# Two merge-gate groups multiplied during the last attention steps, their projections later, in a planned eight-core decoder trunk

## The chip, the cores and the metric

The kernel runs on the eight cores of one Trainium2 chip. Each core takes one of the eight sequences of the batch and shares nothing with the others but the weights that all of them read from device memory. The metric is device time in microseconds (us), of the slowest of the eight cores; lower is better. Engines are named as in the profile: PE multiplies matrices (PEld is its loading of weights), DVE does elementwise arithmetic, ACT evaluates functions, POOL and SP here mostly issue transfers.

## The reference, cut to what matters

Two layers, each on x of 2048 tokens by 2048 channels per core:

```python
shift, scale, gate = split(c_act @ w_ada + b_ada)          # adaLN: one vector each per sequence
h    = x * (1 + scale) + shift
proj = h @ w_in                                            # all mixer inputs, and 4 x 2048 merge-gate logits
ys   = (ssd_branch(..), swa_branch(..), shortconv_branch(..), rglru_branch(..))   # A, B, C, D: 1024 channels each
gates = sigmoid(merge.reshape(b, l, 4, d) + b_gate)
m    = sum(gates[:, :, i] * (ys[i] @ w_branch[i]) for i in range(4))
x    = layer_norm(ALPHA * x + gate[:, None] * (m @ w_out))
```

A is a Mamba-2 mixer (SSD) over chunks of 128 tokens, B is attention over a window of 128 tokens with 16 heads and rotary embedding (rope), C is a gated convolution, D a linear recurrence.

## The kernel before

**Units and stages.** A core works through four units: layer 0 on tokens 0 to 1023 and 1024 to 2047, then layer 1 on the same halves. A unit has these stages, and in all of them PE also has large projections to do: the inputs of mixers C and D; the SSD of mixer A, between whose small steps the first merge pass runs (gates and projections of C and D, groups `m0_0` to `m15_0`); attention, in eight pairs of heads (`qg0` to `qg7`); the second merge pass (gates and projections of A and B, groups `m0_1` to `m15_1`); and `m @ w_out` with its layer norm (`out_unit`, `out_last`). A layer norm runs on into the next unit's first stage.

**A group.** A projection of 256 channels over 1024 tokens is done by `wino` with seven products instead of eight, of two times four matmuls of 128x128 by 128x512 each ("a half" is four such matmuls). After the products, in turn, the four results `c11`, `c22`, `c12` and `c21` are taken out of PSUM by ACT and DVE. For a merge group, `use` makes the gate (tanh) of each result, and `fill` multiplies the matching piece of a mixer's output by `w_branch`, which `mix` joins with the gate. `fill` is called by `wino` right behind each result, so a merge group holds its PSUM bank and its turn until the mixer's output is there.

**Attention's last tiles.** The outputs of mixer A, and of B's first four head pairs, are parked in device memory (`yd_scr`, `yb_scr`) and fetched back by `yload` on SP's queue, as 16 and 8 tiles, before the second merge pass. `rope` swaps halves of a head over partitions by four small transfers (SBUF to SBUF, `arena<-arena`) and then multiplies on DVE.

**adaLN.** Of layer 1's 96 pieces of `w_ada` (and 32 of layer 0's gate) each is one 512 KB transfer on SP's queue and two DVE multiply-adds; after eight pieces `ada_fin` sums over partitions with four small matmuls on PE. `ada_bg(cnt, step)` spreads them: 64 pieces, one each 15 us, in units 0 and 1.

**What sets the order.** The order of every engine's instructions is fixed when the program is built. `Prog.live` plays the program through with fixed costs per operation and per transfer (`DMA_RATE`, `DMA_LAT`, `SLACK`) and lets each free engine take the ready operation of the smallest key. A key is a planned time within the unit (`k0 + TC + ...`) less an advance (`HI`); generators such as `mg`, `yload` or `ada_bg` hand over work when the plan comes to their key. On the chip each engine goes through its list in that order, and waits on semaphores where a predecessor isn't done. All tiles are parts of one tensor `arena`, and PSUM is `ps`, so the profile's names are `arena` and `ps`; lines L705, L709, L713 are the helpers of ACT activations, DVE tensor-tensor and DVE multiply-add operations, L736 and L741 those of matmuls and transposes, L329 that of transfers.

The softmax here doesn't subtract the row's maximum and nothing guards it: scores larger than these inputs give would overflow.

## Time and profile before

| | us |
|---|---|
| median of 3 runs | 5914.43 (5913.79 to 6663.6) |
| profiled execution, its own time | 5964.13 |
| its span on the slowest core, core 7 | 5963.1 |
| PE busy in that span | 5615.3 (94%) |
| DVE busy | 4187.6 (70%) |
| ACT busy | 2842.6 (48%) |
| weight loads on PE | 2570.3 |

The page is of the slowest core. All four units are read from one profiled execution: unit 0 runs from about 152 to 1644 us, unit 1 to 3112, unit 2 to 4526 and unit 3 to the end. The first 150 us load adaLN and x, with little for PE to do. In a table of stretches, the stretch's length less the PE's busy time is PE's idle time; PEclk is the granted share of full clock.

### The profile page before, as it was taken

Reading aid. Unit: us, or ns where it says so; the run is one execution under the profiler, and the core shown is the slowest. Engines: PE = TensorE matmul, PEld = TensorE weight load, DVE = VectorE, ACT = ScalarE, POOL = GpSimd, SP = SyncE. Lnnn points to the kernel's source line nnn. Section 1 sums busy time; section 2 is a strip of 40 time slices with the busy share of each in tenths; the row PEclk is TensorE's granted clock in tenths of the full one; section 3 lists DMA queues with packets and bytes.
Section 4 is the critical chain, followed back from the end, with each engine's and each line's share of the span. In section 5 each row is a group of like instructions: output and inputs, shape, how many; then the busy total and the mean of one; then the engine's idle time right before and its main releaser. Section 6 shows DMA issues by size and latency. Waiting matters only on the chain.

```text
span 5963.1 us, 85339 instructions; the slowest of 8 cores (5863.3 to 5963.1 us)
## 1 busy us (share of the span) xinstructions
PE 5615.3 (94%) x28680; PEld 2570.3 (43%) x28680; DVE 4187.6 (70%) x6902; ACT 2842.6 (48%) x4518; POOL 323.0 (5%) x563
## 2 busy tenths in 40 slices
PE   1999888989999998999999999999999999998998
PEld 1444434434444444444444444444444444443445
DVE  7787866756588787775668767766558767776556
ACT  1565654433156565443326656644324656644224
POOL 0000000000000000000000000000000000000004
PEclk9999999999999999999999999999999999999999
DMA  9667767577566575767656566766756556665554
GB/s 300 124 134 138 145 131 169 131 168 182 166 159 132 122 149 134 163 141 181 157 173 146 97 110 126 134 134 137 181 165 156 106 94 115 118 137 114 115 117 148
DMA packets 251823, 856.94 MB, mean 144 GB/s; under 512 B 27776, under 2 KB 91392, under 8 KB 206848
## 3 DMA queue, kind: packets, MB, share of 16 engines
q0 software_dynamic: 64672, 411.20, 40.1%
q1 hardware_dynamic: 184416, 423.51, 23.6%
q10 hardware_dynamic: 2304, 16.78, 0.9%
q8 instruction: 234, 3.83, 0.3%
q14 instruction: 197, 1.61, 0.1%
HBM read 1133.32 MB, written 120.85 MB: 210 GB/s over the span
## 4 chain that ended last, share of the span: by engine, by line
PE 86%; DMA 5%; DVE 4%; issue 3%; ACT 2%; SPq 1%; DVEq 0%; ACTq 0%; POOL 0%; POOLq 0%
PE ps L736 85%; ACT arena L705 2%; DVE arena L709 2%; DMA arena<-w_ada 2%; DVE arena L713 2%; DMA arena<-arena 1%; PE ps L741 1%; SPq L329 1%; DMA mp_scr<-arena 0%; DMA arena<-x 0%; DMA arena<-cum_scr 0%; DMA arena<-wb 0%; DMA yd_scr<-arena 0%; ACT L705 0%; DMA arena<-yb_scr 0%
## 5 line engine op out<-in xcount | busy, mean ns | idle before, releaser
L736 PE MATMUL ps<-arena 128*128 128x512 bf16 (+6 forms) x27976 | 5588.4, 367 | 315.3 <-DVE arena L709 104.8
L736 PEld LDWEIGHTS ps<-arena 128*128 128x128 bf16 (+3 forms) x27976 | 2510.7, 101 | 3303.6 <-issue 817.9
L709 DVE TENSOR_TENSOR arena<-arena 128x1024 bf16<-128x1024 bf16 (+9 forms) x3052 | 1991.9, 689 | 271.3 <-ACT arena L705 161.3
L705 ACT ACTIVATE arena<-arena 128x512 f32<-128x512 f32 (+9 forms) x2356 | 1395.2, 633 | 1403.4 <-DVE arena L709 814.9
L709 DVE TENSOR_TENSOR arena<-ps,arena 128x512 f32<-128x512 f32 (+5 forms) x1491 | 707.7, 492 | 571.8 <-PE ps L736 496.0
L705 ACT ACTIVATE arena<-ps 128x512 f32<-128x512 f32 (+4 forms) x838 | 534.8, 645 | 668.9 <-PE ps L736 565.5
L713 DVE SCALAR_TENSOR_TENSOR arena<-arena 128x1024 f32<-128x1024 f32 (+3 forms) x765 | 760.0, 1005 | 114.2 <-ACT arena L705 66.8
L713 DVE SCALAR_TENSOR_TENSOR arena<-arena,ps 128x512 f32<-128x512 f32 (+1 forms) x640 | 403.9, 642 | 577.3 <-PE ps L736 528.1
L705 ACT ACTIVATE ps<-ps 128x512 f32<-128x512 f32 x624 | 363.6, 583 | 573.3 <-PE ps L736 524.0
L705 ACT ACTIVATE arena<-ps,arena 128x512 f32<-128x512 f32 (+1 forms) x456 | 312.3, 685 | 347.2 <-PE ps L736 318.6
L705 ACT ACT_TABLE_LOAD x238 | 305.4, 1283 | 99.9 <-DVE arena L709 50.9
L329 POOL DMA_DIRECT2D arena<-w x184 | 97.7, 531 | 2728.7 <-PE ps L736 2003.9
L713 DVE SCALAR_TENSOR_TENSOR arena<-ps,arena 128x512 f32<-128x512 f32 (+1 forms) x153 | 104.9, 687 | 160.5 <-PE ps L736 157.6
L329 POOL DMA_DIRECT2D arena<-wg x128 | 67.7, 529 | 2054.8 <-PE ps L736 1962.4
L709 DVE TENSOR_TENSOR ps<-ps,arena 128x512 f32<-128x512 f32 (+1 forms) x222 | 147.6, 665 | 13.6 <-ACT arena L705 0.5
L741 PE MATMUL ps<-arena 128*128 128x128 bf16 (+1 forms) x704 | 102.0, 245 | 15.9 <-DVE arena L709 11.6
L329 POOL DMA_DIRECT2D arena<-wb x128 | 67.8, 531 | 704.2 <-DVE arena L709 290.4
L741 PEld LDWEIGHTS ps<-arena 128*128 128x128 bf16 (+1 forms) x704 | 69.2, 116 | 72.2 <-issue 31.0
L709 DVE TENSOR_TENSOR arena<-arena,ps 128x256 f32<-128x256 f32 (+1 forms) x172 | 74.7, 445 | 22.6 <-PE ps L736 18.4
L727 DVE RECIPROCAL arena<-arena 128x4 f32<-128x4 f32 (+3 forms) x144 | 72.4, 504 | 11.7 <-ACT arena L705 5.6
L709 POOL TENSOR_TENSOR arena<-arena 128x256 f32<-128x256 f32 (+1 forms) x81 | 71.6, 909 | 97.4 <-ACT arena L705 96.7
L1604 DVE TENSOR_TENSOR_SCAN arena<-arena 128x1024 f32<-128x1024 f32 x32 | 74.1, 2314 | 0.7
(18 smaller groups left out, 85.0 us busy)
## 6 DMA issues: line engine op xcount, KB each, us to landing
arena<-w POOLq DMA_DIRECT2D x184, 1024.0 KB, 10.0
arena<-wg POOLq DMA_DIRECT2D x128, 1024.0 KB, 10.1
arena<-w_ada SPq DMA_DIRECT2D x128, 512.0 KB, 7.3
arena<-wb POOLq DMA_DIRECT2D x128, 512.0 KB, 11.1
arena<-x SPq DMA_DIRECT2D x64, 512.0 KB, 5.4
mp_scr<-arena SPq DMA_DIRECT2D x64, 512.0 KB, 8.4
arena<-cum_scr SPq DMA_DIRECT2D x128, 256.0 KB, 7.3
arena<-mp_scr SPq DMA_DIRECT2D x64, 512.0 KB, 10.8
```

The source lines that it names most:

```text
L329: eng.dma_start(out=o.fn[0], in_=o.fn[1]).then_inc(s, 16)
L705: return P.op("act", lambda e: e.activation(out=out, in_=in_, func=func, **kw), reads, writes, cost=cost, acc=acc, tbl=tbl, hi=hi)
L709: return P.op(eng, lambda e: e.tensor_tensor(out=out, in0=in0, in1=in1, op=op), reads, writes, cost=0.2 + n * 2.1e-3 if eng == "pool" else ...
L713: return P.op("dve", lambda e: e.scalar_tensor_tensor(out=out, in0=in0, scalar=scalar, in1=in1, op0=op0, op1=op1), reads, writes, cost=c_d ...
L727: P.op("dve", lambda e: e.reciprocal(out=out, in_=in_), reads, writes, cost=0.13 + n * 6.3e-3)
L736: r = e.matmul(out, lhsT=lhsT, rhs=rhs, start=st, stop=sp_, skip_group_check=True)
L741: P.op("pe", lambda e: e.transpose(out=out, in_=in_, identity=ident), reads, writes, cost=cost, acc=acc)
L1604: P.op("dve", lambda e: e.tensor_tensor_scan(out=c, data0=a, data1=xs, initial=init, op0=ALU.mult, op1=ALU.add), [ra, rxs] + ri, cv.r, cos ...
```

## The change

It does six things. The planner's transfer rate goes from 280 to 325 GB/s, so it takes every transfer as shorter. `ROPEL` goes from 8 to 0: rope's multiplies, which wait for the swap transfers, get a key that is 8 us earlier. `LNSTEP` goes from 9 to 7: the layer norm of one unit is handed out faster into the next unit's start. `ada_bg` hands out 48 pieces each 20 us in unit 0, 64 each 15 us in unit 1 and 16 each 24 us in unit 2, instead of 64 and 64. The first two groups of the second merge pass (`dc < LAZY`) get a key 30 us earlier (`M1E`). And these two no longer call `fill` in `wino`: a generator `later` calls it for the four results in turn, once the gate of each is there. `LATEM` is empty and changes nothing. The rest of the arithmetic is the same, and each engine has as many operations as before. The whole order is planned anew.

```diff
-    DMA_RATE = 280e3
+    DMA_RATE = 325e3
...
-    ROPEL, HL, ADAL = 8.0, 6.0, 15.0
+    ROPEL, HL, ADAL = 0.0, 6.0, 15.0
...
-        cons = {"c11": c11, "c22": lambda c, q, r: use(1, 1, c, q, r, ALU.add),
+        cons = {"c11": c11, "has": lambda k: SLOT[k] in G, "c22": lambda c, q, r: use(1, 1, c, q, r, ALU.add),
...
-    LNSTEP = 9.0
+    LNSTEP = 7.0
...
+    LAZY = 2
+    M1E = 30.0
+    ADAN = ((48, 20.0), (64, 15.0), (16, 24.0))
...
         def mg(k, dc, p):
             cons, fill, load = merge(l, n, dc, p)
-            group(k, "m%d_%d" % (dc, p), wg_in[l, dc, p], cons, 2.8, fill)
+            if p and dc < LAZY:
+                done = cons.pop("done")
+
+                def later():
+                    for q in ("c11", "c22", "c12", "c21"):
+                        while not cons["has"](q):
+                            yield POLL
+                        yield from fill(q)
+                        yield P.key + 2.8
+                    done()
+                go(later(), k + 2.0)
+            group(k, "m%d_%d" % (dc, p), wg_in[l, dc, p], cons, 2.8, None if p and dc < LAZY else fill)
             go(load(), k - 20.0)
...
-            mg(k0 + TC + s2 * dc, dc, 1)
+            mg(k0 + TC + s2 * dc - (M1E if dc < LAZY else 0.0), dc, 1)
...
-        if n < 2:
-            go(ada_bg(64, 15.0), k0 + 30.0)
+        if n < 3:
+            go(ada_bg(*ADAN[n]), k0 + 30.0)
```

**Place 1: PE, seventh head pair of unit 0.** In PE's list, 128x256 and the following 128x128 on L736 are products of queries and keys (QK), 128x65 are products of the probabilities with the values (PV), L741 128x128 are transposes of the result, and 128x512 are halves of projections. Before:

```order
L736 MATMUL ps<-arena 128x65 x6
L736 MATMUL ps<-arena 128x256 x4
L741 MATMUL ps<-arena 128x128 x2
L736 MATMUL ps<-arena 128x128 x2
L736 MATMUL ps<-arena 128x65 x10
L736 MATMUL ps<-arena 128x256 x2
L741 MATMUL ps<-arena 128x128 x4
L736 MATMUL ps<-arena 128x256 x4
L736 MATMUL ps<-arena 128x512 x4
```

The same steps now, from the QK of four key blocks on:

```order
L736 MATMUL ps<-arena 128x256 x4
L736 MATMUL ps<-arena 128x512 x4
L736 MATMUL ps<-arena 128x65 x8
L736 MATMUL ps<-arena 128x512 x8
L736 MATMUL ps<-arena 128x65 x2
L736 MATMUL ps<-arena 128x512 x8
L741 MATMUL ps<-arena 128x128 x2
L736 MATMUL ps<-arena 128x512 x4
L736 MATMUL ps<-arena 128x65 x6
L736 MATMUL ps<-arena 128x128 x2
L736 MATMUL ps<-arena 128x512 x4
L741 MATMUL ps<-arena 128x128 x2
```

Halves of `m0_1` and `m1_1` have moved in between these steps, where seven rows stood with none.

**Place 2: PE, the first wait for the tiles that `yload` fetches, unit 0.** `s_dve` and `s_act` are waits for DVE and ACT, `d_sp_` numbers are waits for transfers on SP's queue, here the tiles of `yd_scr`, and `d_pool_` one on POOL's. Before, the wait stood behind the last transposes of the last head pair:

```order
L741 MATMUL ps<-arena 128x128 [waits s_dve]
L741 MATMUL ps<-arena 128x128
L736 MATMUL ps<-arena 128x512 x4
L736 MATMUL ps<-arena 128x512 [waits s_act]
L736 MATMUL ps<-arena 128x512 x7
L736 MATMUL ps<-arena 128x512 [waits d_sp_49,d_sp_47,d_sp_45,d_sp_43,d_pool_2]
L736 MATMUL ps<-arena 128x512 x3
L736 MATMUL ps<-arena 128x512 [waits d_sp_50,d_sp_48,d_sp_46,d_sp_44]
```

Now it stands within the last head pair's steps, ahead of its third QK:

```order
L741 MATMUL ps<-arena 128x128 [waits s_dve]
L741 MATMUL ps<-arena 128x128
L736 MATMUL ps<-arena 128x512 [waits d_sp_33,d_sp_31,d_sp_29,d_sp_27,d_pool_0]
L736 MATMUL ps<-arena 128x512 x7
L736 MATMUL ps<-arena 128x256 [waits s_act]
L736 MATMUL ps<-arena 128x256 x3
L736 MATMUL ps<-arena 128x65 [waits s_dve]
L736 MATMUL ps<-arena 128x65 x7
```

The transposes at the head of the second fence are those of the seventh head pair's end, not the eighth's: the wait has moved forward past most of one head pair. From the QK in place 1 on, 64 matmuls of 128x512 stood ahead of it, and 40 do now.

**Place 3: PE, third group of heads in the SSD of unit 0.** L741 128x128 are the transposes that open a chunk, 128x256 on L736 is the product that makes a chunk's state, which needs what DVE makes of those transposes, 128x1 is `ada_fin`. Before:

```order
L736 MATMUL ps<-arena 128x512 x8
L736 MATMUL ps<-arena 128x1 x4
L741 MATMUL ps<-arena 128x128 x2
L736 MATMUL ps<-arena 128x128
L736 MATMUL ps<-arena 128x256
L741 MATMUL ps<-arena 128x128 x2
L736 MATMUL ps<-arena 128x128
L736 MATMUL ps<-arena 128x512 x32
```

Now:

```order
L736 MATMUL ps<-arena 128x512 x4
L741 MATMUL ps<-arena 128x128 x2
L736 MATMUL ps<-arena 128x128
L736 MATMUL ps<-arena 128x512 x20
L736 MATMUL ps<-arena 128x256
L736 MATMUL ps<-arena 128x512 x8
L741 MATMUL ps<-arena 128x128 x2
L736 MATMUL ps<-arena 128x128
```

Between the transposes of chunk 5 and the product of its state there are five halves now, and there were none; `ada_fin` stands elsewhere.

## Rows read from the trace of the kernel before

**Rows 1.** Span and mean granted clock: the slowest core, and each die's median.

```profile
core 7: 5963.1 us, clock 0.971
die 0 (median of its cores): 5902.5 us, clock 0.983
die 1 (median of its cores): 5938.7 us, clock 0.976
```

**Rows 2.** Busy time by stretch, SSD of units 0 to 3, and the columns.

```profile
core 7: us, PE busy (x) PEld busy (x) DVE busy (x) ACT busy (x) POOL busy (x), PEclk, DMA share, GB/s
468.30:955.80 487.50, 431.34 (x2148) 197.46 (x2147) 355.91 (x630) 272.11 (x490) 22.93 (x44) 0.93 0.71 141
...
1980.00:2434.10 454.10, 421.52 (x2160) 193.86 (x2159) 355.86 (x617) 273.71 (x508) 18.75 (x36) 0.96 0.65 138
...
3431.70:3858.50 426.80, 411.00 (x2113) 188.76 (x2112) 313.06 (x557) 269.65 (x493) 22.91 (x44) 0.97 0.68 122
...
4845.90:5261.90 416.00, 409.41 (x2135) 188.76 (x2134) 318.15 (x553) 273.63 (x510) 18.74 (x36) 0.98 0.63 115
```

**Rows 3.** The same view, last two head pairs to the third merge group, units 0 to 3.

```profile
1158.40:1262.10 103.70, 81.72 (x478) 36.87 (x476) 66.32 (x141) 36.24 (x48) 4.23 (x8) 0.87 0.69 166
...
2637.40:2729.60 92.20, 78.00 (x472) 35.90 (x471) 61.05 (x128) 35.83 (x47) 4.78 (x9) 0.91 0.74 171
...
4056.50:4142.80 86.30, 77.11 (x453) 34.65 (x452) 54.51 (x117) 35.13 (x47) 4.24 (x8) 0.92 0.74 165
...
5469.50:5560.80 91.30, 75.99 (x463) 34.51 (x462) 56.56 (x116) 36.04 (x47) 4.22 (x8) 0.91 0.68 154
```

**Rows 4.** The same view: second merge pass of unit 0, and starts of units 1 and 2.

```profile
1262.10:1644.60 382.50, 382.46 (x1888) 175.40 (x1887) 224.83 (x367) 108.92 (x170) 13.19 (x25) 1.00 0.69 173
1644.60:1980.00 335.40, 326.73 (x1478) 139.41 (x1477) 288.70 (x366) 201.07 (x280) 13.20 (x25) 0.94 0.64 142
...
3112.90:3431.70 318.80, 316.25 (x1461) 135.46 (x1460) 254.70 (x318) 197.10 (x265) 16.28 (x31) 0.97 0.61 120
```

**Rows 5.** In order of time, unit 0's seventh head pair: start, us, instruction, [idle before <-releaser].

```profile
1197.07 1.02 ACT L705 ACTIVATE arena<-ps 128x1024 bf16<-128x1024 f32 x1
...
1200.46 3.17 DVE L709 TENSOR_TENSOR arena<-arena 128x1024 f32<-128x1024 f32 x4 [3.15 <-DMA arena<-arena]
...
1202.43 0.71 PE L736 MATMUL ps<-arena 128*128 128x65 bf16 x10 [3.90 <-DVE arena L709]
...
1203.68 0.68 DVE L709 TENSOR_TENSOR arena<-arena 128x1024 bf16<-128x1024 bf16 x1
```

**Rows 6.** In order of time, SP's queue at the same place (rope's copies, `yload`).

```profile
1191.53 2.37 SPq L329 DMA_DIRECT2D arena<-arena  x4
...
1208.29 15.98 SPq L329 DMA_DIRECT2D arena<-yd_scr  x16
1224.31 3.75 SPq L329 DMA_DIRECT2D arena<-yb_scr  x8
```

**Rows 7.** Transfers issued from 1200 to 1245 us: median time to landing last.

```profile
arena<-yd_scr SPq DMA_DIRECT2D x16, 128.0 KB, 11.4
```

**Rows 8.** Waits from 1190 to 1245 us: total, times, longest.

```profile
PE ps L736 <- DMA arena<-yb_scr: 7.5, 1, 7.5
```

**Rows 9.** Busy time by stretch, within the SSD of unit 0.

```profile
800.00:850.00 50.00, 27.63 (x127) 12.20 (x125) 31.90 (x65) 21.88 (x43) 0.50 (x1) 0.73 0.38 95
```

**Rows 10.** Waits from 800 to 850 us.

```profile
PE ps L736 <- DVE arena L713: 8.6, 2, 7.4
...
DVE arena L713 <- DMA arena<-w_ada: 6.0, 1, 6.0
```

**Rows 11.** The chain of waits at that place: start, us, what.

```profile
788.73 21.30 DMA arena<-w_ada
```

**Rows 12.** DVE's groups by shape, rope's and adaLN's: count | busy, mean ns | idle before.

```profile
L709 DVE TENSOR_TENSOR arena<-arena 128x1024 f32<-128x1024 f32 x240 | 289.0, 1218 | 48.3 <-DMA arena<-arena 38.0 <-ACT arena L705 9.9
...
L713 DVE SCALAR_TENSOR_TENSOR arena<-arena 128x512 f32<-128x512 f32 x374 | 276.9, 744 | 42.4 <-DMA arena<-w_ada 27.8 <-DVE arena L713 2.8 <-DVE arena L709 0.3
```

**Rows 13.** Busy time by stretch: two short ones at a lower granted clock.

```profile
286.25:292.69 6.44, 6.44 (x27) 2.68 (x25) 5.37 (x7) 5.06 (x8) 0.00 (x0) 0.81 0.94 163
842.74:849.57 6.83, 3.00 (x14) 1.30 (x15) 4.87 (x9) 3.69 (x9) 0.00 (x0) 0.50 0.00 1
```

More of the change, by code:

```diff
@@ L1641, in locked @@
         return g()
+    SLOT = {"c11": (0, 0), "c22": (1, 1), "c12": (0, 1), "c21": (1, 0)}
     def merge(l, n, dc, p):
@@ L1663, in fill @@
         def fill(k):
-            i, ti = {"c11": (0, 0), "c22": (1, 1), "c12": (0, 1), "c21": (1, 0)}[k]
+            i, ti = SLOT[k]
             while "wb" not in G or any(ydone[b] < 8 * (n + 1) for b in ((1, 4) if pair[i] == 1 else (pair[i],))):
@@ L2046, in build_program @@
     GX = (6, 7)
+    LATEM = ()
+    LAZY = 2
+    M1E = 30.0
+    ADAN = ((48, 20.0), (64, 15.0), (16, 24.0))
     groups = []
@@ L2104, in mg @@
             cons, fill, load = merge(l, n, dc, p)
-            group(k, "m%d_%d" % (dc, p), wg_in[l, dc, p], cons, 2.8, fill)
+            if p and dc < LAZY:
[9 more added lines that the diff above has]
+            group(k, "m%d_%d" % (dc, p), wg_in[l, dc, p], cons, 2.8, None if p and dc < LAZY else fill)
             go(load(), k - 20.0)
         for dc in range(16):
-            mg(k0 + TA + 12.0 + SM * dc, dc, 0)
+            mg(k0 + TA + 12.0 + SM * dc if dc < 16 - len(LATEM) else k0 + TC + LATEM[dc - 16], dc, 0)
         def dopen(m):
```

## The prediction

> **What bounds the kernel now.** I read the cores first: core 7 is the slowest, and its die has the lower clock [rows 1]. Then I cut its span by stages and took each stretch's PE busy time from its length. The second merge pass shows what the kernel does at its best: of 382.50 us PE idles 0.04, at granted clock 1.00, 382.46 us for 1888 matmuls, so 0.203 us a matmul and 0.81 us a half [rows 4]. PE bounds that stretch, and nothing but fewer matmuls would shorten it. Idle time sits elsewhere. The SSD of units 0 to 3 has 56.2, 32.6, 15.8 and 6.6 us of it (111.2), the ends of attention 22.0, 14.2, 9.2 and 15.3 (60.7) [rows 2, 3]. The number of matmuls is nearly the same in each of the four, so work does not explain the differences. Units 0 and 1 carry the adaLN pieces, 2 and 3 none. In these stretches PE waits for chains through ACT and DVE: the chain, not a busy engine, sets the pace. Since every matmul has to be done anyway and the merge pass behind has no gap, a microsecond of idle time removed ahead of it comes off the end, and none can be made good there.
>
> Two things add to it. The granted clock of the four ends is 0.87, 0.91, 0.92 and 0.91, against 1.00 in the merge pass [rows 3, 4]; stretches at 0.50 (1.2 GHz) lie behind idle time, as at 842.74 us [rows 13]. And DVE goes through its list in order, so a late transfer in it stops everything behind it: rope's multiplies waited 38.0 us for their swaps, adaLN's 27.8 us for `w_ada` [rows 12].
>
> **The change, part by part.** All sums are made on the profiled execution, 5964.13 us; the median of the runs is 49.7 us lower, and I take off the same microseconds there.
>
> *Ends of attention.* One step from QK to PV takes 1.02 us on ACT and 0.68 us on DVE [rows 5], with the handing over some 2.3 us, my estimate. Place 1 had no halves in seven rows; now one or two (0.81 to 1.62 us) stand between most dependent steps. That covers between a third and two thirds of a step, and where DVE itself is late, as at 1202.43, where PE idled 3.90 us behind a swap [rows 5], it covers only its own length. Bounds: nothing, if DVE stays the one that is late; all 60.7 us. I take 60%, nearer to the step than to the late swap: **-36 us**. The clock: missing share times PE busy time is 0.13 x 81.72 + 0.09 x 78.00 + 0.08 x 77.11 + 0.09 x 75.99 = 30.6 us [rows 3]; part of the low clock lies in idle time, so I count half, and 60% of it goes: **-9** (0 to -31).
>
> *The new wait.* Place 2 is what speaks against the change. PE's first wait for the `yd_scr` tiles now stands inside the last head pair's steps, and that pair's QK, PV and transposes are queued behind it; ACT and DVE then wait for those. Before, the tiles were issued over 15.98 us from 1208.29 on [rows 6] and took 11.4 us [rows 7]. The wait needs the seventh of 16, issued at about 1208.3 + 6/16 x 16.0 = 1214.3, landed at about 1225.7. PE came to it at about 1228, some 25 matmuls before the 7.5 us that it then waited for `yb_scr` until 1240.7 [rows 8]. Now 40 rather than 64 matmuls of projections stand between place 1 and the wait: 24 x 0.203 = 4.9 us earlier, and up to 14 us earlier as the 9 us of gaps at place 1 close too. With 2 us in hand, that is 3 to 12 us of waiting, if the tiles are issued no earlier. They may be: rope's last swaps were issued at 1191.53 [rows 6], 16.8 us before the tiles, and the tiles stand right behind them in the list but for two or three transfers; then the wait is 0. Bounds 0 to 12 us a unit; I take 5, near the middle: **+20** over four units. As a price from a page, the Trainium skill (DMA: Bandwidth & Descriptors, Anatomy of one DMA) has a fixed cost of about 2 us and 436 GB/s: a 128 KB tile would land in about 2.3 us, an estimate by that page, and this term would be nothing. The trace does not agree: 11.4 us is the median here, with the other transfers beside it.
>
> *SSD of units 0 and 1.* The 50 us from 800 on hold 22.4 us of unit 0's 56.2 [rows 9]. 7.4 of them are `ada_fin` behind a `w_ada` piece that landed 21.30 us after its issue [rows 10, 11]; the rest are steps that stood without a half between them, as in place 3, and there now are five halves. So 22.4 - 7.4 = 15 go. The other 33.8 us go with the pieces: 48 in place of 64 in unit 0, a quarter: 8.5. Unit 1 keeps 64 pieces and gets a replanned order: 4 of its 32.6. Together **-27** (between 0, if new late pieces take their place, and -76, if both came to unit 3's 6.6). The clock (0.93 and 0.96, partly at 0.81) gives back about a quarter of 0.07 x 431 = 30: **-7**.
>
> *Sixteen adaLN pieces in unit 2.* Their DVE work (two multiply-adds of 0.744 us each [rows 12], 24 us in all) lies beside PE's projections; unit 1's start, with pieces, idles 8.7 us, unit 2's, without, 2.6 [rows 4]. About 20 pieces cost 6.1, so 16 cost **+5** (0 to 5).
>
> *Layer norm in 7 us steps.* DVE is busy 288.70 of 335.40 us at the start of unit 1 [rows 4], and the same work is handed out in 112 rather than 144 us. It is covered while PSUM is emptied in time; without that cover the 8.7 us could double in three units. I take **+3** (0 to 26).
>
> *Rope's key.* The multiplies now stand at the first place at which the plan has the swaps landed, with less other DVE work ahead of them. The waits were 38.0 us [rows 12]. Bounds: none more, or as much again. I take half, 19 us on DVE, of which 40% reaches PE, as halves now stand between: **+8**.
>
> *Transfer rate, opening, output.* The merge passes and the output projection have no PE idle time to lose or win; their cover is the weights' lead of 70 us in the plan. The opening keeps its transfers, and I cost it at nothing (3 us either way).
>
> **The sum** is -36 - 9 + 20 - 27 - 7 + 5 + 3 + 8 = -43 us: 5921 us on the profiled execution, 5914.4 - 43 = **5871 us** as a median, 0.7% less.
>
> **The rivals.** *The gain is eaten.* The new waits stand at 12 us a unit (+28 to the sum) and rope's waits double with PE behind them (+11 more): -4, about 5910 us. For it: PE and DVE both go in order, and every late transfer of [rows 12] stopped PE. Against: the attention list has halves in it now.
>
> *Everything closes.* The ends lose all 60.7 us and 15 of clock, the SSDs come down to unit 3's 6.6 (-76) and 10 of clock, and no new wait appears: -161, about 5753 us. For it: unit 3 does the same SSD in 416.0 us [rows 2]. Against: adaLN is still in units 0 and 1, and late pieces cost 5 to 7 us each.
>
> *Slower: the wait for `yd_scr` decides.* Place: place 2, in each of four units. Up to 5 us a unit it is in the sum; the total is no faster from 5 + 43/4 = 16 us a unit on, which is one more late landing like that of 21.30 us [rows 11] in each unit. At 25 us a unit the time is 5914 + 4 x 9 = 5950 us. Against: in unit 0, the worst shown, the tiles were all but there.
>
> *A lower clock.* If denser work on PE in SSD and attention were granted only 0.81, as at 286.25 us [rows 13], the four ends (373.5 us, PE busy 312.8) would pay about 312.8 x (1/0.81 - 1/0.90) = 39 us and the gain would go: about 5910 us. The merge pass, the densest stretch, shows 1.00 [rows 4], so I give it 2 in 100. The Trainium skill (TensorE: Matmul & The Clock Gate, Seeing it yourself) says that three or more cores of a die with dense matmuls are held at 13/16 of full clock for as long as the load lasts. By that page the merge pass should show 0.81; it does not, and the trace decides.
>
> *The change does nothing.* PE could find the same idle time at other places of the new order: 5914, within the first rival.
>
> **How the numbers follow.** The sum and its neighbourhood (gain of 20 to 80 us) 0.57; the gain eaten (within 20 us of before, the lower clock with it) 0.22; more than 80 us 0.13, of which over 118 us 0.05; slower by more than 20 us 0.08, of which over 118 us 0.02. A difference of 2%, 118 us, is about what a measurement here can tell from no change. So faster by over 2% 0.05, within 0.93, slower 0.02. The range runs from 5800 (all of the ends, half of the SSDs' bound) to 5930 (new waits of about 20 us a unit); by the cases about 0.06 lie below and 0.07 above.
>
> **What would show it.** In the changed profile the four ends should idle about 24 us in place of 60.7, and 20 more at the `yd_scr` wait, as PE waiting for that transfer; unit 0's SSD about 33, unit 1's 29; unit 2's start about 7; DVE's wait for the swaps about 57. I am wrong if PE's wait for `yd_scr` is over 10 us in several units, if unit 0's SSD keeps its 56 us with other late pieces, or if the start of units 1 to 3 idles over 25 us in all.

## The result and the profile after

The median of the changed kernel is 5863.34 us and the mean of the executions compared 5860.5 us, against 5914.1 us of the kernel before on the same chip: a ratio of 0.9909, 95% interval 0.9881 to 0.9938, so 37 to 70 us less. That is under 2%, and the interval excludes no change. The forecast was 43 us less. In some executions, of either kernel, one die or both run at a lower clock and the time is longer, often by hundreds of us; all comparisons here leave those out, and of e8 and e9, profiled in such an execution, only the other die is read.

The page's core, core 6, lacks 551 of its 28,680 matmul records, so the rows below are of core 5, on the same die and 8 us shorter. Span and mean granted clock of the changed kernel, to be read beside [rows 1]:

```profile
core 5: 5845.1 us, clock 0.988
core 6: 5853.3 us, clock 0.988
...
die 0 (median of its cores): 5831.9 us, clock 0.990
die 1 (median of its cores): 5841.1 us, clock 0.989
```

The same stretches as in [rows 2 to 4], columns as there: SSD of units 0 and 1, the four ends of attention, the second merge pass of unit 0, the starts of units 1 and 2.

```profile
457.30:917.50 460.20, 417.49 (x2145) 192.09 (x2144) 343.20 (x611) 269.82 (x491) 22.93 (x44) 0.97 0.72 142
...
1124.40:1216.00 91.60, 78.90 (x459) 35.44 (x458) 58.82 (x124) 34.31 (x46) 2.64 (x5) 0.93 0.74 176
1216.00:1600.00 384.00, 382.75 (x1887) 175.30 (x1886) 229.69 (x372) 110.09 (x171) 14.26 (x27) 1.00 0.69 174
1600.00:1911.70 311.70, 305.46 (x1454) 132.76 (x1453) 283.72 (x359) 197.64 (x276) 13.21 (x25) 1.00 0.68 148
1911.70:2357.10 445.40, 421.16 (x2182) 194.48 (x2181) 353.12 (x612) 271.18 (x501) 18.73 (x36) 0.98 0.68 142
...
2558.70:2647.90 89.20, 77.98 (x472) 35.70 (x471) 61.27 (x127) 34.76 (x46) 3.50 (x7) 0.96 0.75 178
...
3031.20:3355.10 323.90, 311.23 (x1470) 134.88 (x1469) 269.72 (x345) 198.38 (x265) 16.29 (x31) 0.99 0.66 140
...
3975.60:4056.60 81.00, 74.22 (x451) 33.59 (x450) 54.70 (x117) 34.32 (x46) 2.46 (x5) 0.98 0.66 155
...
5361.00:5445.70 84.70, 76.42 (x465) 34.69 (x464) 54.77 (x119) 34.67 (x45) 3.12 (x6) 0.96 0.70 154
```

Length less PE busy gives the idle time. On these two cores the ends come to 12.7 + 11.2 + 6.8 + 8.3 = 39.0 us, where they had 60.7 [rows 3], and their clock rose from 0.87 to 0.92 to 0.93 to 0.98. SSD of units 0 and 1 idles 42.7 and 24.2 us, where it had 56.2 and 32.6 [rows 2]. Unit 1's start idles 6.2 (8.7 before), unit 2's 12.7 (2.6 before) [rows 4]. The merge pass idles 1.3 us (0.04 before), at clock 1.00.

One core of one execution is a thin basis for stages that differ by a few us. So the same reading was made on every core whose record is complete (six of the eight in each run; three in e8 and e9) and the idle times averaged. These means stand in the table (of the merge passes' 21 to 28 us, 18 to 20 are the output's end in every kernel); its last column is the ratio of the times with its interval, or, where too few runs were left for an interval, their number and their median beside that of the kernel before in the same rounds. Rounds ran on several chips: the kernel before took 5913 to 5923 us in most and 5930 in those of e9 to e12, so times are compared with the kernel before in the same rounds.

| kernel | SSD unit 0 | SSD unit 1 | start unit 2 | four ends | merge passes and output | all idle | time against before |
|---|---|---|---|---|---|---|---|
| before | 52.2 | 39.2 | 3.3 | 57.9 | 21.2 | 347.5 | 1 |
| changed | 36.9 | 21.5 | 10.2 | 31.5 | 22.1 | 302.1 | 0.9909 (0.9881 to 0.9938) |
| e1 before, early groups alone | 56.5 | 32.4 | 5.4 | 30.1 | 22.4 | 328.2 | 0.9952 (0.9933 to 0.9972) |
| e5 before, rate 325 alone | 58.1 | 33.9 | 3.9 | 65.2 | 21.3 | 377.2 | 1.0056 (1.0036 to 1.0075) |
| e8 before, rate 325 and new adaLN | 40.4 | 32.9 | 6.5 | 62.8 | 23.1 | 368.5 | one run, 5940 against 5923 |
| e2 changed, no early groups | 37.8 | 22.0 | 7.9 | 64.1 | 22.5 | 342.3 | two runs, 5900 against 5916 |
| e3 changed, early but not later | 40.6 | 29.2 | 10.2 | 40.7 | 28.0 | 331.1 | 0.9990 (0.9972 to 1.0007) |
| e4 changed, rate 280 | 45.1 | 37.0 | 9.8 | 21.7 | 23.7 | 333.6 | 0.9994 (0.9980 to 1.0008) |
| e6 changed, adaLN as before | 59.0 | 22.5 | 0.6 | 21.6 | 22.7 | 300.1 | 0.9879 (0.9855 to 0.9903) |
| e7 changed, rope's key as before | 39.0 | 21.9 | 9.7 | 32.6 | 22.7 | 315.2 | 0.9918 (0.9897 to 0.9939) |
| e9 changed, 28 us early | 41.9 | 30.5 | 8.2 | 39.0 | 23.4 | 339.8 | one run, 5892 against 5930 |
| e10 changed, 3 us more for `cum_scr` | 47.7 | 29.9 | 9.6 | 25.2 | 22.8 | 319.4 | one run, 5873 against 5930 |
| e11 changed, layer norm step 9 | 41.1 | 29.6 | 8.0 | 33.3 | 22.1 | 337.9 | 0.9963 (0.9944 to 0.9983) |
| e16 changed, tiles 10 us earlier | 35.8 | 31.1 | 6.2 | 30.3 | 22.1 | 311.1 | one run, 5870 against 5913 |
| e17 changed, unit 2's pieces later | 43.7 | 22.6 | 0.6 | 35.0 | 25.0 | 315.0 | two runs, 5865 against 5923 |

From before to changed the idle time falls by 45.4 us, of which the ends give 26.4 and SSD 33.9 (15.3 in unit 0, 17.7 in unit 1); the start of unit 2 takes back 6.9, and attention ahead of its last two head pairs 11.6 (16.8 to 28.4). PE's busy time falls too, from 5572 to 5531 us, by the granted clock; the profiled execution of before took 50 us longer than the median, so no more than a part of that is the change's.

### The profile page after: what moved, and what is told of

It reads as the page before. It is cut to its first block, busy times and chain, and to the rows that moved or that the text cites. A ratio compares the mean times of both kernels' runs of the same rounds, so it can differ in the third digit from the quotient of the medians.

```text
span 5853.3 us, 84743 instructions; the slowest of 8 cores (5822.8 to 5853.3 us)
## 1 busy us (share of the span) xinstructions
PE 5497.7 (94%) x28129; PEld 2545.5 (43%) x28680; DVE 4178.1 (71%) x6902; ACT 2835.4 (48%) x4518; POOL 322.9 (6%) x563
## 3 DMA queue, kind: packets, MB, share of 16 engines
q0 software_dynamic: 64672, 411.20, 40.7%
q1 hardware_dynamic: 184416, 423.51, 24.1%
## 4 chain that ended last, share of the span: by engine, by line
PE 78%; DMA 10%; DVE 5%; issue 4%; ACT 3%; SPq 1%; DVEq 0%; ACTq 0%; POOL 0%; POOLq 0%
PE ps L736 77%; DVE arena L709 3%; ACT arena L705 3%; DMA arena<-cum_scr 2%; DVE arena L713 2%; DMA arena<-arena 2%; DMA yd_scr<-arena 1%; DMA arena<-w_ada 1%; DMA arena<-wb 1%; PE ps L741 1%; DMA arena<-w 1%; DMA arena<-x 1%; SPq L329 1%; DMA arena<-x_scr 1%; ACT L705 0%
## 5 line engine op out<-in xcount | busy, mean ns | idle before, releaser
L736 PE MATMUL ps<-arena 128*128 128x512 bf16 (+6 forms) x27425 | 5472.5, 363 | 328.9 <-DVE arena L713 103.9
L736 PEld LDWEIGHTS ps<-arena 128*128 128x128 bf16 (+4 forms) x27976 | 2487.0, 100 | 3223.8 <-issue 612.5
L709 DVE TENSOR_TENSOR arena<-arena 128x1024 bf16<-128x1024 bf16 (+8 forms) x3052 | 1998.6, 693 | 297.2 <-ACT arena L705 176.5
L705 ACT ACTIVATE arena<-ps 128x512 f32<-128x512 f32 (+5 forms) x838 | 533.7, 644 | 666.8 <-PE ps L736 556.4
L713 DVE SCALAR_TENSOR_TENSOR arena<-arena 128x1024 f32<-128x1024 f32 (+2 forms) x765 | 760.1, 1009 | 92.4 <-ACT arena L705 56.7
L329 POOL DMA_DIRECT2D arena<-w x184 | 97.7, 531 | 2635.7 <-PE ps L736 1986.6
L741 PE MATMUL ps<-arena 128*128 128x128 bf16 (+1 forms) x704 | 101.0, 243 | 10.2 <-DVE arena L709 5.3
L741 PEld LDWEIGHTS ps<-arena 128*128 128x128 bf16 (+1 forms) x704 | 69.4, 115 | 67.2 <-issue 26.1
```

Of the source, the lines that this page charges most:

```text
L329: eng.dma_start(out=o.fn[0], in_=o.fn[1]).then_inc(s, 16)
L705: return P.op("act", lambda e: e.activation(out=out, in_=in_, func=func, **kw), reads, writes, cost=cost, acc=acc, tbl=tbl, hi=hi)
L709: return P.op(eng, lambda e: e.tensor_tensor(out=out, in0=in0, in1=in1, op=op), reads, writes, cost=0.2 + n * 2.1e-3 if eng == "pool" else ...
L713: return P.op("dve", lambda e: e.scalar_tensor_tensor(out=out, in0=in0, scalar=scalar, in1=in1, op0=op0, op1=op1), reads, writes, cost=c_d ...
L736: r = e.matmul(out, lhsT=lhsT, rhs=rhs, start=st, stop=sp_, skip_group_check=True)
L741: P.op("pe", lambda e: e.transpose(out=out, in_=in_, identity=ident), reads, writes, cost=cost, acc=acc)
```

## The experiments

Each edit is to the changed kernel unless it says "before". Every edit has the whole order planned anew; what that does by itself is one of the questions.

### Do the early groups shorten the ends?

e1 gives them to the kernel before, alone (`LAZY`, `M1E`, `later`); e2 takes them from the changed kernel; e3 keeps the early key and calls the projections in the group.

```diff
# e2
-    LAZY = 2
+    LAZY = 0
# e3
-    LAZY = 2
+    LAZY = 0
-            mg(k0 + TC + s2 * dc - (M1E if dc < LAZY else 0.0), dc, 1)
+            mg(k0 + TC + s2 * dc - (M1E if dc < 2 else 0.0), dc, 1)
```

> The kernel before with one part of the change alone: groups m0_1 and m1_1 get their key 30 us earlier and their projections are called later; transfer rate, rope's key, layer norm step and adaLN stay as before. My theory (the early groups fill the dependent steps of attention's end): idle PE time in the four ends falls from about 60 us to 35 to 40, SSD keeps its 111 us, the time is 5885 to 5895 us. Rival (the gain came from the other parts and the new order): the ends keep about 60 us and the time is 5905 to 5915 us.

> The changed kernel without early groups (all sixteen groups of the second merge pass at their old keys, projections in their groups). My theory: the ends of attention go back to about 60 us idle from about 39, and nothing else moves: about 5863 + 25 = 5888 us. Rival (early groups are not what shortens it): 5863 us within 8 us.

> The changed kernel with the two groups 30 us early, but their projections called in the group as before, behind each result. My theory (both parts are needed): the first projection waits for the tiles of yd_scr with its PSUM bank and the group's turn held, so fewer halves stand between the attention steps; ends idle 45 to 60 us, 5875 to 5895 us. Rival (the early key alone does it): ends idle about 39 us, 5863 us within 8 us.

The windows of e1, core 5: SSD of unit 0 and the ends of units 0 to 3.

```profile
460.90:946.50 485.60, 424.36 (x2148) 195.88 (x2147) 356.02 (x630) 271.76 (x490) 22.93 (x44) 0.94 0.71 142
...
1147.30:1220.60 73.30, 68.28 (x445) 31.66 (x443) 57.78 (x128) 34.88 (x47) 3.17 (x6) 1.00 0.84 203
...
2588.80:2670.40 81.60, 76.13 (x502) 35.63 (x501) 65.16 (x142) 36.27 (x48) 3.70 (x7) 1.00 0.84 206
...
3991.50:4085.20 93.70, 77.82 (x451) 35.30 (x450) 56.36 (x119) 34.94 (x47) 4.23 (x8) 0.91 0.73 161
...
5396.50:5476.50 80.00, 74.69 (x464) 34.00 (x463) 54.95 (x116) 34.95 (x46) 2.64 (x5) 0.98 0.66 156
```

The ends of units 0, 1 and 3 idle 5.0, 5.5 and 5.3 us, at clock 0.98 to 1.00. That of unit 2 idles 15.9 us at 0.91, and 13.3 in the means, where the kernel before had 10.0: in this order the early groups did nothing there. SSD gains nothing as a whole (61.2 us here in unit 0; over four units 113.2 in the means, 112.9 before). So the part works alone, on the ends, and is worth 0.5%. Without it (e2, e5, e8, before) the ends idle 58 to 65 us, with it (all other rows but e3) 22 to 39.

e3 came out between its theory and its rival: ends of 40.7, near the rival's 39, and the time of before, slower than either forecast. So the early key alone gives most of what the ends gain (64.1 in e2, 40.7 in e3, 31.5 in the changed kernel), and merge passes that idle 6 us more take some of it back. That the first results hold their PSUM banks until the tiles are there, with `fill` in the group, is not shown: PE's waits for the tiles sum to 0 to 3.9 us a core in e3, and in the merge passes of units 1 and 2 it waits for ACT instead (core 5):

```profile
PE ps L736 <- ACT arena L705: 5.2, 2, 4.3
...
PE ps L736 <- ACT arena L705: 7.2, 3, 4.7
```

What the later call adds beyond the early key rests on this one order, and a later call without the early key was not run.

### Does the new wait for `yd_scr` cost what I put on it?

```diff
# e16
-        go(yload(), k0 + TC - 16.0)
+        go(yload(), k0 + TC - 26.0)
```

> The changed kernel with the transfers of the yd_scr tiles 10 us earlier in the plan. If my new wait is set by when they are issued: PE's waits for yd_scr in units 1 and 3 (4.4 and 4.0 us on one core) go to under 1 us, and the ends idle about 27 us in place of 31. Rival (the queue ahead of them sets their issue): the waits stay.

PE's waits for the tiles in the changed kernel, core 5, at the ends of units 1 and 3 (there are none in units 0 and 2). Core 5 has the most of them: of the six cores read, cores 1, 2 and 3 have none, cores 4 and 7 have 1.0 and 3.0 us, and the mean is 2.1 us.

```profile
PE ps L736 <- DMA arena<-yd_scr: 4.4, 2, 2.2
...
PE ps L736 <- DMA arena<-yd_scr: 4.0, 1, 4.0
```

SP's queue of the changed kernel, unit 0, beside [rows 6]:

```profile
1161.00 3.35 SPq L329 DMA_DIRECT2D arena<-arena  x4
...
1166.35 9.59 SPq L329 DMA_DIRECT2D arena<-yd_scr  x16
```

The tiles are issued 5.4 us behind rope's last swaps, where it was 16.8 [rows 6], and in 9.6 us. They moved ahead with PE's wait. In e16 the waits do not go. On the same core they are (its whole span):

```profile
PE ps L736 <- DMA arena<-yd_scr: 7.0, 2, 5.0
```

But core 5 is not typical: over the six cores e16 waits 6.7 us on average, three times as long as the changed kernel. Its queue in unit 1, core 5:

```profile
2583.85 12.23 SPq L329 DMA_DIRECT2D arena<-yd_scr  x12
...
2605.11 4.68 SPq L329 DMA_DIRECT2D arena<-arena  x4
```

In units 0, 2 and 3 the tiles still stand right behind the last swaps (3.0 to 4.7 us on core 5), so there the earlier key changed nothing. In unit 1 twelve of the sixteen went ahead of the last swaps, and there the wait is 5.0 us on this core, the larger part of its 7.0. So the forecast that the waits go is refuted; the rival's reason, that the queue ahead sets the issue, fits three units of four.

### What shortened SSD: the rate, adaLN, or the order?

```diff
# e4
-    DMA_RATE = 325e3
+    DMA_RATE = 280e3
# e5, in the kernel before: DMA_RATE = 325e3;  e8: that, and ADAN as in the change
# e6
-    ADAN = ((48, 20.0), (64, 15.0), (16, 24.0))
+    ADAN = ((64, 15.0), (64, 15.0))
# e9
-    M1E = 30.0
+    M1E = 28.0
# e10, the transfer of cum_scr in ssd
-                  writes=[cus[v][1]], nbytes=262144, hi=30.0)
+                  writes=[cus[v][1]], nbytes=262144, hi=30.0, slack=5.0)
```

> The changed kernel planned with the old transfer rate of 280 GB/s. My prediction costed the rate at nothing: 5863 us within 8 us. Rival A (the higher rate puts consumers too near to their transfers: DVE's and ACT's waits for cum_scr grew from about 35 to 75 us in the changed kernel): those waits fall back to about 40 us, SSD idles 10 to 20 us less, 5845 to 5853 us. Rival B (the higher rate is what shortened SSD, by letting the plan start things earlier): SSD idles 110 us again and the time is about 5890 us.

> The kernel before with the transfer rate of 325 GB/s alone. Theory A (the rate by itself shortens SSD, as the run with 280 in the changed kernel suggests, where SSD idled 110 us again): SSD idles about 80 us in place of 113, ends stay at about 60, time 5880 to 5890 us. Theory B (the rate and the new adaLN spacing are needed together): SSD stays at 100 to 113 us, time 5905 to 5915 us.

> The changed kernel with adaLN handed out as before, 64 pieces each 15 us in units 0 and 1, none in unit 2. My prediction: unit 0's SSD gets about 8.5 us more idle time for its 16 pieces, unit 2's start 5 to 10 us less, about 5863 us in all. Theory B above: unit 0's SSD goes from about 37 back to 50 us, unit 2's start to about 3: 5865 to 5875 us.

> The kernel before with the transfer rate of 325 GB/s and adaLN in 48, 64 and 16 pieces, nothing else. Theory A: as the run with the rate alone, less the unit-0 adaLN pieces. Theory B: only now SSD falls, to about 80 us idle, with the ends at 60: 5885 to 5895 us. If both this run and the one with the rate alone keep about 110 us in SSD, neither theory stands and SSD's gain is one order among many that happen to differ.

> The changed kernel with the two early groups 28 instead of 30 us early: a change that should do nothing in itself, but has the whole order planned anew. It measures what a new order alone does. Theory A (a new order is worth a few us): 5855 to 5872 us, each stage's idle time within 5 us of the changed kernel's. Theory B (the order is the larger part, and differences of 20 to 40 us between single edits say little about the edit): more than 15 us away from 5863, with single stages off by 10 us or more.

> The changed kernel planned with 3 us more for each cum_scr transfer and nothing else, so SSD's consumers of these transfers are placed later. Theory A (the higher rate shortens SSD because these transfers land earlier in the plan): DVE's and ACT's waits for cum_scr fall from about 75 to under 40 us, but SSD idles about 100 us again as with the rate of 280, 5880 to 5900 us. Theory B (the waits on the chip are what is left of SSD's idle time): with the waits SSD falls too, to 60 to 70 us, 5845 to 5855 us.

**The rate has no sign of its own.** Taken from the changed kernel it costs nearly all of the gain (0.9994), given to the kernel before it makes it slower (1.0056). Rival B for e4, that the rate shortens SSD, is refuted by e5: SSD of unit 0 idles 58.1 there. Its trace does show what it does directly: with transfers planned shorter, their consumers are placed nearer. ACT's waits for `cum_scr` over the whole span, in the kernels before, changed, e4 and e10 (core 7 of before, else core 5):

```profile
ACT arena L705 <- DMA arena<-cum_scr: 35.6, 12, 8.1
```

```profile
ACT arena L705 <- DMA arena<-cum_scr: 83.8, 21, 12.7
```

```profile
ACT arena L705 <- DMA arena<-cum_scr: 21.4, 11, 6.5
```

```profile
ACT arena L705 <- DMA arena<-cum_scr: 35.7, 11, 14.2
```

But e4 and e10, with the short waits, idle more in SSD (110.4 and 97.7 us over four units) than the changed kernel with the long ones (79.0). So in these orders shorter waits for `cum_scr` bought nothing.

**A new order by itself is worth tens of us.** e9 changes a key by 2 us, which should mean nothing in itself. Its SSD, core 1, units 0 and 1:

```profile
456.50:922.20 465.70, 421.86 (x2145) 193.08 (x2144) 342.79 (x610) 269.92 (x489) 22.92 (x44) 0.96 0.72 139
...
1914.90:2374.80 459.90, 429.88 (x2207) 198.66 (x2206) 363.78 (x631) 278.63 (x516) 18.74 (x36) 0.96 0.71 143
```

43.8 and 30.0 us idle, 9 more in unit 1 than in the changed kernel; in the means all idle time is 38 us more. In time it is one run, 29 us over the changed kernel's 5863, of which some 16 are its rounds' (the kernel before took 5930 there, not 5914). That is nearer to theory B than to A, though no single stage is off by the 10 us that B asked for: SSD of the four units together is off by more than 20, the ends by 7.5. e11 is the firmer case, with an interval clear of the changed kernel's, if its own edit does nothing. So a single edit that moves the time by 15 to 35 us has shown little about itself. What can be trusted is what repeats over many orders.

**What repeats is unit 0's SSD.** Wherever adaLN hands out 64 pieces each 15 us, it idles 52 to 66 us (six kernels with e12 and e15 below, mean 57.9); wherever 48 each 20 us, 36 to 48 (eleven kernels, mean 40.9). In the kernel before with the new rate it goes from 58.1 to 40.4 by the new spacing alone (e5, e8); e8 gains nothing as a whole, since its ends idle 62.8 us and SSD of units 1 to 3 67 (42 in the changed kernel). The transfers of `w_ada` issued in that stretch (count; shortest, median and longest issue in ns; the time of the first and the last), and DVE's wait for them, of before, of changed (which has no such wait there) and of e6:

```profile
L329 SPq DMA_DIRECT2D arena<-w_ada x29: 327/333/1982, 498.1 to 953.1; - x29
```

```profile
DVE arena L713 <- DMA arena<-w_ada: 19.0, 4, 6.2
```

```profile
L329 SPq DMA_DIRECT2D arena<-w_ada x22: 328/333/1364, 476.3 to 900.0; - x22
```

```profile
L329 SPq DMA_DIRECT2D arena<-w_ada x29: 327/333/628, 484.1 to 926.8; - x29
```

```profile
DVE arena L713 <- DMA arena<-w_ada: 25.7, 6, 7.5
```

Seven pieces fewer, and DVE's 19 to 26 us of waiting for late ones are gone. So it is in all kernels of the two groups, on the one core read of each: 18 to 26 us of these waits with 64 pieces, 0 to 6 with 48. PE's idle time differs by 17 us between the groups. The total does not show it: e6, with the old spacing, is as fast as the changed kernel, since its unit 2 starts 10 us better and its ends and attention idle less.

Unit 1's SSD has 64 pieces each 15 us in every kernel of the table, and its idle time runs from 21.5 to 39.2 all the same. Some of that repeats: the four kernels built on before (before, e1, e5, e8) idle 32 to 39 us there, mean 34.6, and e4 37.0; the twelve others (with e12 and e15 below) 22 to 32, mean 26.7. So of the 17.7 us that the change gained there, about 8 seem to come with the changed kernel's keys at a rate of 325 or more. Neither did it alone: e5 and e8 have the rate, e4 the keys. Which key it is, is not shown. The rest is the draw of one order.

### Late transfers or DVE's work, and where else could the pieces go?

e15 is e6 with the multiply-adds of a piece 10 us later in the plan (`ADAL` 25 for 15). e13 and e14 give `ada_bg` a list of stretches per unit and leave SSD out, but for six pieces in unit 1; e14 changes nothing else, e13 also has rate 345 and 28 us. e17 moves only unit 2's sixteen into its attention (early groups 33 us). e18 spreads them thinly, with rate 345. e12 has no new idea: e6 with 345 and 33 us.

```diff
# e14: (start, pieces, step) within a unit
-    ADAN = ((48, 20.0), (64, 15.0), (16, 24.0))
+    ADAN = (((30, 16, 18), (770, 14, 16), (1010, 26, 12)),
+            ((20, 18, 16), (330, 6, 70), (765, 16, 15), (1030, 16, 17)), ((800, 16, 20),))
```

> The changed kernel with adaLN's pieces taken out of SSD and put where PE has no idle time to lose: unit 0 has 16 at its start, 14 in attention and 26 in the second merge pass, unit 1 18, 6 in SSD, 16 in attention and 16 in the merge pass, unit 2 16 from attention on; transfer rate 345 GB/s, early groups 28 us ahead. Theory A (pieces in SSD cost idle time): SSD of units 0 and 1 falls to near unit 2's 15 us each from about 37 and 22, unit 2's start to about 3 from 10; merge passes stay near 0: 5825 to 5840 us. Rival (the merge passes pay for it, with transfers or memory late): the merge passes of units 0 and 1 idle 10 us or more each: 5855 to 5880 us.

> The same spreading of adaLN with transfer rate 325 GB/s and early groups 30 us ahead, so that only the places of the pieces differ from the changed kernel. Theory A: SSD of units 0 and 1 near 15 us each, as in the run with 345: 5830 to 5845 us. Theory C (each new order brings its own 20 us, and SSD's idle time is such a draw): SSD of the two units differs from the run with 345 by 15 us or more in all.

> The changed kernel with adaLN as before (64 pieces each 15 us in units 0 and 1) and their multiply-adds placed 10 us later than before. If late transfers of w_ada are what makes SSD wait: DVE's wait for w_ada falls from about 40 us to under 20 and unit 0's SSD from 59 to about 40 us. If the pieces' DVE work and places in the order are: the waits fall, and unit 0's SSD stays at 55 to 60 us.

> The changed kernel with unit 2's sixteen pieces moved from its start into its attention (early groups 33 us ahead, all else the same). If the terms add up: unit 2's start idles 3 us in place of 10, the rest as in the changed kernel or as in its like with 28 us: 5855 to 5885 us, with SSD of unit 0 at 33 to 41 us. If attention pays for them: unit 2's attention idles 7 us more and the total gains nothing.

> adaLN spread thinly: unit 0 has 16 pieces at its start, 18 in SSD, 8 in attention, 14 in the merge pass, unit 1 18, 12, 10 and 16, unit 2 16 in the merge pass; transfer rate 345 GB/s. If the cost of a piece grows with its density: SSD of unit 0 idles 28 to 35 us, of unit 1 about 20, unit 2's start 3, merge passes 3 to 8 each in place of 20: 5840 to 5860 us. If merge passes pay as much as before: 5865 to 5880 us.

> A version put together from the runs so far: early groups 33 us ahead, adaLN as before (nothing in unit 2), transfer rate 345 GB/s. By the runs: ends about 22 to 32 us, unit 2's start about 1 in place of 10, SSD of unit 0 near 59 with 64 pieces, unit 1 near 22: 5845 to 5865 us. Rival (each new order brings its own 20 us): 5865 to 5885 us.

| kernel | SSD unit 0 | SSD unit 1 | start unit 2 | merge passes and output | all idle | time against before |
|---|---|---|---|---|---|---|
| e13 | 24.1 | 19.2 | 3.7 | 51.9 | 308.9 | 0.9896 (0.9809 to 0.9983) |
| e14 | 23.2 | 20.2 | 5.3 | 60.5 | 321.3 | two runs, 5873 against 5913 |
| e15 | 55.4 | 31.6 | 0.6 | 22.6 | 327.4 | 0.9941 (0.9888 to 0.9993) |
| e18 | 41.6 | 30.7 | 1.5 | 50.7 | 332.4 | 0.9956 (0.9938 to 0.9974) |
| e12 | 66.0 | 28.3 | 2.1 | 34.0 | 348.0 | two runs, 5912 against 5930 |

e13 and e14 agree within 2 us in SSD, though their orders differ: without pieces, unit 0's SSD idles 23 to 24 us, so they are what costs there. In unit 1 it is not so: with 6 pieces its SSD idles 19 and 20 us, where the changed kernel, with 64 each 15 us, idles 21.5. The merge passes pay for it, most where 26 pieces went (unit 0: 25 and 20 us idle); with 16 pieces, unit 1's idles 22 us in e14 and under 7 in e13, so that price too depends on the order. Unit 0's merge pass of e14, core 5, and PE's waits in it:

```profile
1185.40:1601.50 416.10, 393.12 (x1919) 179.63 (x1918) 260.42 (x428) 109.82 (x170) 14.39 (x27) 0.98 0.78 197
```

```profile
PE ps L736 <- DVE arena L709: 8.5, 3, 5.0
PE ps L736 <- ACT arena L705: 8.2, 5, 5.2
PE ps L736 <- ACT ps L705: 6.2, 3, 4.1
```

23.0 us idle where there was 1, behind ACT and DVE, at 197 GB/s and a DMA share of 0.78 (174 and 0.69 in the changed kernel). A stretch without idle time is not a stretch without a limit.

e15 does not settle lateness against DVE's work: DVE's wait in unit 0's SSD was 18.2 us still, so the later place did not take the waits away, and the idle time stayed at 55.4. e18, with 16 pieces in that SSD, still waited 7.2 us for them and idled 41.6, no less than with 22 pieces that came in time, which speaks for lateness; a kernel with 29 pieces and none late was not made.

e17 takes unit 2's start from 10.2 to 0.6, as expected, and the whole gains nothing that can be told from another order. Nor did e12, put together from the best single numbers. e6 measured lowest (0.9879), but its interval overlaps the changed kernel's: no version beat it clearly.

### Two edits whose own stages do not move

```diff
# e7
-    ROPEL, HL, ADAL = 0.0, 6.0, 15.0
+    ROPEL, HL, ADAL = 8.0, 6.0, 15.0
# e11
-    LNSTEP = 7.0
+    LNSTEP = 9.0
```

> The changed kernel with rope's key 8 us later, as before. My prediction (+8 for the earlier key): DVE's wait for the swaps falls from about 50 to 33 to 40 us, attention's first six pairs idle about 17 us in place of 28, 5853 to 5858 us. Rival (the waits for swaps are not set by the key): the same waits, 5863 us within 8 us.

> The changed kernel with the layer norm step of 9 us as before. My prediction (+3 for the step of 7): starts of units 1 to 3 idle 3 us less, about 5860 us. Rival (the faster step is what lets unit 1's SSD open earlier): unit 1's SSD goes from about 22 to 32 to 39 us idle, 5873 to 5880 us.

DVE's multiplies that wait for rope's swaps, core 5, in the changed kernel and in e7, to be read beside [rows 12]:

```profile
L709 DVE TENSOR_TENSOR arena<-arena 128x1024 f32<-128x1024 f32 x240 | 290.2, 1223 | 62.8 <-DMA arena<-arena 54.5 <-ACT arena L705 7.8 <-issue 0.4
```

```profile
L709 DVE TENSOR_TENSOR arena<-arena 128x1024 f32<-128x1024 f32 x240 | 289.9, 1221 | 64.1 <-DMA arena<-arena 55.6 <-ACT arena L705 7.4 <-issue 0.9
```

54.5 and 55.6 us: here the key decides nothing. In e5, with the old key and the new rate, it is 48.4; in e1, with the old key and rate, 26.4; in e6, new key and rate, 31.1. Neither the key nor the rate alone orders these. In e11 the starts of units 1 and 3 idle 7.7 and 2.4 us against 6.3 and 2.4, so the step costs nothing there either way. But e11 is slower than the changed kernel, beyond both intervals, and what it lacks stands in SSD (unit 1: 29.6 against 21.5, unit 3: 17.8 against 6.2). That can be a new order, as in e9 and e10; the rival written down before the run, that the faster step lets unit 1's SSD open earlier, is not excluded by one order.

## The prediction, step by step

**The chances: a step that failed.** I took 2%, 118 us, as about what a measurement can tell from no change, and put 0.93 on a result within it, beside a sum of -43. The two kernels' compared times lie within 1 and 9 us of each other (5913.8 and 5914.4; 5854.8 to 5863.9), and the interval, 37 to 70 us, excludes no change. The sum said faster, and it was; the chances had hidden that.

**Ends: the mechanism right, two sizes off.** -36 + 20 = -16 was the forecast for their idle time, and -26.4 came; for the clock I had -9, and PE's busy time there fell by 5 us on the cores of the rows and by 9 in the means. The two sizes erred in opposite ways. Without the new wait the ends idle 31.5 - 2.1 = 29.4 us in the means where 24 was the forecast, so the halves covered half of the idle time, not 60%. e1 and e2 give it to the early groups.

**The new wait: the term was too large.** +20 against 2.1 us in the mean of six cores, 8.4 on the worst of them, nothing in two units of four. The step that failed took the tiles' issue as fixed and moved only PE, and settled near the middle; the lower bound, that they come right behind the swaps, was what happened (5.4 us behind). The rival that needed 16 us a unit there fell with it. The tiles' landing time hardly changed: 9.8 us at the median over the whole changed kernel on core 5, 10.8 over the kernel before on core 7. The Trainium skill (DMA: Bandwidth & Descriptors, Anatomy of one DMA — SWDGE (gpsimd) path) gives its two costs for transfers that GpSimd issues; the estimate of 2.3 us that I made from them for tiles on SP's queue is not borne out by this trace either. That the term came near nothing is due to the issue, not to a faster landing.

**SSD: the size near, the reasons wrong.** -27 was the forecast, -33.9 came. Unit 0 lost 15.3, where I had 8.5 for the pieces and 15 for steps that now have halves between them; the runs give 17 to the pieces, beside DVE's wait for late ones, and nothing that repeats to the steps. For unit 1 I had 4 and 17.7 came, of which about 8 repeat in other orders. The failed step is the price of a piece, taken as in proportion to their number.

**Unit 2's pieces: right.** +5 against +6.9; e6 and e17, without them there, idle 0.6.

**Layer norm, rope: wrong in kind.** +3 and +8 were priced as effects of `LNSTEP` and `ROPEL`. The starts of units 1 and 3 idle 2.6 us less than before, not 3 more. DVE's wait for the swaps came as forecast (57 against 54.5) and attention ahead of the ends lost 11.6 us, but in e7, with the old key, both are as long (55.6, and 31.7 us idle against 28.4): the key is not the cause, and what is stays open.

**The rate: a term that was missing.** I costed it at nothing, reasoning from where PE has idle time to lose. It moves the time by 33 us the one way (e5) and by 50 the other (e4), through the order as a whole.

**The clock.** -9 - 7 = -16 was the forecast. Idle time fell by 45.4 us and the time by 53.6, so about 8 us are left for the clock; that is an estimate, since the two figures are of different executions.

**The rivals.** The lower clock is refuted here: the ends' clock rose. "Everything closes" fell in SSD. For "the gain is eaten" I had argued that every late transfer stops PE; ACT's longer waits for `cum_scr` beside a shorter SSD speak against that. It was not this order's fate, but nearly that of e3 and e4, which differ from it by one number or by the later call. None of the three signs of being wrong came: PE's wait for `yd_scr` was at most 8.4 us over all units, unit 0's SSD idled 36.9, the starts of units 1 to 3 18.9 in all.

**How far the total was luck.** Seven kernels have the change's early groups with `later`, its rate and no more than 48 pieces in unit 0, and differ in what is small or showed no effect in its own stage (changed, e7, e9, e10, e11, e16, e17). By the table they are 54, 49, 38, 57, 22, 43 and 59 us faster than before: 46 on average, from 22 to 59, three of them by a single run. The forecast of 43 lies among them, but its terms were off in both directions: for idle time alone they come to -27, where -45.4 came. That the sum ended near was in part luck, and it could not have been right about one order to better than some 20 us.

## What to carry to other kernels

Where a planner orders everything, an edit's own effect is what repeats over several orders of the same parts: make a control that changes the plan and nothing else before you read a difference of less than 1%, and read by stage rather than by total. Independent work put between dependent steps pays (e1, e2); whether it must also give back its bank and its turn before what it needs arrives rests on one order (e3). Background transfers can cost in a stage of dependent chains far out of proportion to their number, and where they did, some came late (whether lateness is the cause was not settled); moved into a stage that is full, they can make that one wait.

## What was not expected

A key moved by 2 us left 38 us more idle time (e9), as much as most parts of the change are worth, though the time was only some 13 to 16 us worse beside the kernel before. The merge pass, which idles 1 us at clock 1.00 with 174 GB/s, idled 23.0 us at 197 GB/s with 26 pieces more, though PE's waits there are for ACT and DVE and none is for a transfer (e14). And ACT's waits for `cum_scr` could more than double, from 35.6 to 83.8 us on the cores shown, while SSD became shorter.
